# Another order of the 36 steps of the routed experts, with the single-expert steps spread among the others

## The chip, the cores and the metric

The kernel runs on one core of a Trainium2 chip. The metric is the device time of one execution in microseconds (us), median of the runs shown. Engines: PE multiplies (PEld loads its stationary operand), DVE and ACT do elementwise work, POOL (GpSimd) issues the indirect transfers of this stage, SP issues the transfers of the dense weights.

## The reference, cut to what matters

Two blocks of a network run one after the other on 256 tokens of width 1024. The change lies in the routed experts of the first block:

```
_, e_idx = lax.top_k(jnp.where(expert_mask, biased, -jnp.inf), TOP_K)     # 8 of 64 experts for each of 256 tokens
...
def expert_block(args):
    xb, e = args
    return (jax.nn.silu(xb @ w_gate[e]) * (xb @ w_up[e])) @ w_down[e]
...
routed = jax.ops.segment_sum(yb * row_gate[:, None], row_tok, num_segments=T + 1)[:T]
```

An expert's gate and up weights are 1024 x 512 numbers together (2.10 MB in f32), its down weights 256 x 1024 (1.05 MB), 3.15 MB in all. There are 2048 pairs of token and expert. Evaluating the reference's routing on its own inputs gives these token counts, sorted: 157, 93, 91, 88, 86, 82, 73, 65, 59, 56, 53, 49, and so on down to 1, 1, 0, 0. So two experts have no token, and one has more than 128.

## The kernel before, in words

**Steps and sets.** The routed experts are computed in 36 steps of 128 rows each. Experts are ranked by their token count while the kernel runs, and a *set* is one expert's weights in one of six buffers. A *solo* step (S, 8 of them) gives all 128 rows to one of the 8 best-filled experts: one set. A *mixed* step (X, 16) holds one expert of ranks 8 to 23 in 64 rows, one of ranks 24 to 39 in 32 rows, and 32 rows for an overflow: three sets. A *narrow* step (Z, 12) holds two experts of ranks 40 to 63 and two overflows, in 32 rows each: four sets. That makes 104 sets. Whether an overflow is used depends on the data: an expert gets overflow rows only for tokens beyond its 128, 64 or 32 rows. With the counts above only one overflow is used (the expert with 157 tokens), and it is the first overflow, which belongs to the first mixed step. The requests for the other 39 overflow sets and for the two experts without tokens are issued all the same, but every index in them is out of bounds, so they move no weights. The two experts without tokens are those of the last narrow step. So a step moves this many experts' weights: solo 1, mixed 2 (the first one 3), narrow 2 (the last one 0), 63 in all.

**What sets the order.** The string `ORDER` (L116) gives the kind of each step; `sets_of(i)` says which weights step i uses, and set number s goes to buffer s % 6 (`SETS = 6`). `row_of(i)` maps a step to its column in the tables, and the host writes the table of row bases in `_route` from the same string.

**POOL's queue** (L720, L724, L712). Ahead of the loop, sets 0, 1, 2, then 5 and 3, then 4 are requested, and the rows of steps 0 to 2. Then for each step i, in this order: the rows of step i + 3 (`gather`, L712, once the rows of step i have been turned); after PE has done gate and up of step i, gate and up of the sets that reuse that step's buffers (`after_step(i)`, L720); after PE has done down of step i - 1, the down weights of the sets that reuse those (L724). All requests are served in the order in which they are issued.

**PE's order in a step** (L1137, L1156, L1170, L1123, L915): gate and up of step i (waits for all its sets, and for ACT and DVE to have copied the turned rows, L1844 and L2767), down of step i - 1, combine of step i - 2, turning the rows of step i + 1, turning the hidden values of step i. ACT's silu of step i (L1860) comes once in a step, right after gate and up.

```
if after_step(i):
    full(pool, "moe", mu("gu", i))
for s in after_step(i):
    gate_up(s)
```

Of the kernel before, what the change touches and what calls it, by code (L numbers as in the profile page):

```python
# [112 lines left out]
STEPS, W_UNITS, OVER = FIRST_STEP["end"], FIRST_UNIT["end"], FIRST_UNIT["end"] - EXPERTS  # L113
GROUP = 32
SETS = 6
ORDER = [{"S": "solo", "X": "mixed", "Z": "narrow"}[c] for c in "SSZSZSZXXXZZZZXXXXXSZSZZZSZSXXXXXXXX"]  # L116
UNUSED = float(1 << 20)


def row_of(i):  # L120

    return FIRST_STEP[ORDER[i]] + ORDER[:i].count(ORDER[i])


def sets_of(i):

    n = ORDER[:i].count(ORDER[i])
    pair, quad, over = (FIRST_UNIT[name] for name in ("pair", "quad", "over"))
    mixed, narrow = FIRST_STEP["narrow"] - FIRST_STEP["mixed"], STEPS - FIRST_STEP["narrow"]
    return {"solo": [n], "mixed": [pair + n, quad + n, over + n],  # L130
            "narrow": [quad + mixed + 2 * n, quad + mixed + 2 * n + 1, over + mixed + narrow + n, over + mixed + n]}[ORDER[i]]


def groups_of(i):

    cuts = {"solo": [(0, 0, P)], "mixed": [(0, 0, 32), (0, 32, 64), (1, 64, 96), (2, 96, P)],
            "narrow": [(h, GROUP * h, GROUP * h + GROUP) for h in range(4)]}[ORDER[i]]
    return [(first_of(i) + h, slice(at, end)) for h, at, end in cuts]
# [5 lines left out]
def first_of(i):  # L144

    return FIRSTS[i]
# [3141 lines left out]
def _route(np):  # L3288
# [7 lines left out]
    for i in range(STEPS):  # L3296
        for unit, col in {"solo": ((0, 0),), "mixed": ((0, 0), (1, 2 * GROUP)), "narrow": ((0, 0), (1, GROUP))}[ORDER[i]]:
            c[:, ROUTE["base"] + sets_of(i)[unit]] = P * row_of(i) + col
# [66 lines left out]
```

## Time and profile before

| | |
|---|---|
| median of 3 runs | 1881.57 us (1877.88 to 1883.33) |
| profiled execution: its span | 1885.5 us |
| routed steps, first gate and up to last combine | about 534 to 1082 us of the span |
| PE busy over the span | 93% |
| bytes of the software queue (POOL) | 218.10 MB of 414.50 MB |

Of the profiled execution only the span is given. It is 3.9 us over the median of the runs and 2.2 us over the slowest of them. The page has 40 slices of 47.1 us; the routed steps are slices 11 to 23. A time in the rows is counted from the start of the span.

### The profile page before, as it was taken

The numbers are of one execution on the slowest core, as the hardware profiler recorded it, in microseconds if no ns is written. First come the engines' busy times: TensorE is split into PE (matmuls) and PEld (weight loads), VectorE is DVE, ScalarE is ACT, GpSimd is POOL, SyncE is SP. The second block draws the span as 40 slices with busy tenths as digits, with TensorE's granted clock in tenths as the row PEclk, the third lists the DMA queues.
The fourth block names the chain that finished last, engine by engine and source line by source line (L and its number), as shares of the span: only waits on it lengthen the run. The fifth ranks groups of instructions, "written<-read, shape, count | busy, mean of one in ns | idle before, by whom it ended". The sixth has DMA issues, their size and how long they took to land.

```text
span 1885.5 us, 30512 instructions
## 1 busy us (share of the span) xinstructions
PE 1744.2 (93%) x12794; PEld 1265.1 (67%) x12794; DVE 920.3 (49%) x1354; ACT 668.3 (35%) x948; POOL 498.7 (26%) x360
## 2 busy tenths in 40 slices
PE   6999999999899888999998989899997979979998
PEld 3899998786454333444444467678886749968887
DVE  4276933766732111112121378565447775765453
ACT  3455347443311111111111255454434452334442
POOL 1277877100134344434544200000000002400000
PEclk9999999999889998999999989999998989989999
DMA  8455541156689999998799933155554400024542
GB/s 363 180 183 189 187 179 68 67 225 237 271 319 374 388 391 377 390 418 340 267 380 409 396 120 132 67 207 189 200 198 143 172 23 26 4 90 179 180 174 91
DMA packets 64700, 414.50 MB, mean 220 GB/s; under 512 B 20308, under 2 KB 20340, under 8 KB 24256
## 3 DMA queue, kind: packets, MB, share of 16 engines
q0 software_dynamic: 37536, 218.10, 29.3%
q1 hardware_dynamic: 26624, 192.95, 27.6%
q8 instruction: 95, 1.56, 0.3%
q10 hardware_dynamic: 416, 1.66, 0.2%
q14 instruction: 29, 0.24, 0.0%
HBM read 549.99 MB, written 2.10 MB: 293 GB/s over the span
## 4 chain that ended last, share of the span: by engine, by line
PE 78%; DVE 10%; issue 3%; DMA 3%; ACT 2%; another core or an unknown queue 1%; POOL 1%; ACTq 0%; DVEq 0%; POOLq 0%
PE ps L1137 13%; PE ps L827 10%; PE ps L829 10%; PE ps L828 10%; PE ps L1156 6%; PE ps L868 5%; PE ps L869 5%; PE ps L870 5%; PE ps L1170 3%; PE ps L1535 3%; DMA arena<-in_moe_dn,arena 2%; PE ps L886 2%; PE ps L1123 1%; DVE ring_lo L2352 1%; PE ps L1571 1%
## 5 line engine op out<-in xcount | busy, mean ns | idle before, releaser
L828 PE MATMUL ps<-ring_lo,arena_r 128*128 128x512 f32 x888 | 349.4, 393 | 0.0
L1137 PE MATMUL ps<-arena 128*32 128x512 f32 (+1 forms) x896 | 244.0, 614 | 10.3 <-ACT arena L1844 6.1
L1137 PE MATMUL ps<-ring,arena 128*32 128x512 f32 (+1 forms) x752 | 230.0, 614 | 16.8 <-issue 8.7
L870 PE MATMUL ps<-arena_r,ring_lo 128*128 128x256 f32 x768 | 217.3, 283 | 0.0
L827 PE MATMUL ps<-arena_r 128*128 128x512 f32 x528 | 209.5, 397 | 2.7 <-DVE arena_r L2378 2.7
L829 PE MATMUL ps<-arena_r 128*128 128x512 f32 x528 | 206.1, 390 | 0.0
L828 PEld LDWEIGHTS ps<-ring_lo,arena_r 128*128 128x128 f32 x888 | 169.1, 190 | 33.5
L2352 DVE TENSOR_TENSOR ring_lo<-ring,arena_r 128x2048 fp32r<-128x2048 f32 x66 | 150.7, 2291 | 75.2 <-ACT arena_r L1722 75.1
L1722 ACT ACTIVATE high<-ring 128x2048 fp32r<-128x2048 f32 x62 | 118.5, 1915 | 117.2 <-PE ps L868 71.7
L868 PE MATMUL ps<-arena_r,high 128*128 128x256 f32 x528 | 150.9, 286 | 2.4 <-DVE ring_lo L2352 1.3
L869 PE MATMUL ps<-arena_r,high 128*128 128x256 f32 x528 | 149.4, 283 | 0.0
L870 PEld LDWEIGHTS ps<-arena_r,ring_lo 128*128 128x128 f32 x768 | 147.4, 192 | 0.0
L2792 DVE SCALAR_TENSOR_TENSOR arena<-ps,arena 128x256 f32<-128x256 f32 x36 | 17.4, 484 | 262.6 <-ACT arena L1860 262.6
L661 POOL TENSOR_TENSOR ring_lo<-ring,high 128x2048 fp32r<-128x2048 f32 x26 | 120.5, 4634 | 86.6 <-ACT high L1722 86.6
L1722 ACT ACTIVATE arena_r<-ring 128x2048 fp32r<-128x2048 f32 x66 | 126.1, 1920 | 37.6 <-DMA ring<-in_weights 37.6
L1156 PE MATMUL ps<-arena 128*32 128x512 f32 (+1 forms) x448 | 124.2, 620 | 6.7 <-DMA arena<-in_moe_dn,arena 6.7
L1137 PEld LDWEIGHTS ps<-ring,arena 128*32 128x32 f32 (+1 forms) x752 | 66.2, 118 | 94.5 <-issue 93.0
L1137 PE MATMUL ps<-spare,arena 128*32 128x512 f32 x272 | 123.7, 607 | 0.5
L1156 PE MATMUL ps<-ring,arena 128*32 128x512 f32 (+1 forms) x376 | 117.1, 607 | 0.9 <-ACT arena L1868 0.5
L1137 PEld LDWEIGHTS ps<-arena 128*32 128x32 f32 (+1 forms) x896 | 71.2, 120 | 69.8 <-issue 69.7
L827 PEld LDWEIGHTS ps<-arena_r 128*128 128x128 f32 x528 | 99.2, 188 | 22.4 <-issue 3.2
L829 PEld LDWEIGHTS ps<-arena_r 128*128 128x128 f32 x528 | 99.1, 188 | 20.8
(490 smaller groups left out, 3551.7 us busy)
## 6 DMA issues: line engine op xcount, KB each, us to landing
ring<-in_weights SPq DMA_DIRECT2D x183, 1024.0 KB, 4.8
arena<-in_ln POOLq DMA_DIRECT2D x2, 1024.0 KB, 5.1
arena<-in_lora POOLq DMA_DIRECT2D x1, 1152.0 KB, 5.5
arena<-in_x POOLq DMA_DIRECT2D x1, 1024.0 KB, 12.4
h_rows<-arena ACTq DMA_DIRECT2D x1, 1024.0 KB, 12.0
arena<-in_bands POOLq DMA_DIRECT2D x1, 1024.0 KB, 7.5
arena<-in_rw_kk_ka POOLq DMA_DIRECT2D x2, 512.0 KB, 7.8
arena<-in_rw_w0a POOLq DMA_DIRECT2D x1, 1024.0 KB, 4.9
```

The costliest lines, as they stand in the source:

```text
L661: pool.tensor_tensor(ring_lo[:, s, :], ring[:, s, :], hi_of(stage, i).bitcast(F32), ALU.subtract).then_inc(sem(f"w_split{s}"), 1)
L827: head = pe.matmul(dst, hi, w, start=start, stop=False, skip_group_check=True)
L828: pe.matmul(dst, hi, rest, start=False, stop=False, skip_group_check=True)
L829: return head, pe.matmul(dst, lo, w, start=False, stop=stop, skip_group_check=True)
L868: head = pe.matmul(dst, w, hi[:, k, :], start=(k == 0), stop=False)
L869: pe.matmul(dst, w, lo[:, k, :], start=False, stop=False)
L870: mm = pe.matmul(dst, rest, hi[:, k, :], start=False, stop=(k == count - 1))
L1137: mm = pe.matmul(pb("moe", mu("gu", i))[at, :], x_cols[:, k, at], gu_w[s % SETS][:, k * 512:(k + 1) * 512], start=(k == 0), stop=(k == KC ...
L1156: mm = pe.matmul(pb("moe", mu("y", i, n))[at, :], hid_cols[:, i % 2, f, at], dn_w[s % SETS][:, f * D + n * 512:f * D + n * 512 + 512], sta ...
L1170: mm = pe.matmul(ps[:, 2 * t + n, :], places_of[:, i % 2, tokens(t)], part[:, i % 2, n * 512:(n + 1) * 512], start=False, stop=(i == STEPS ...
L1722: fn(hi_of(stage, i), ring[:, s, :], ACT.Copy).then_inc(sem(f"w_hi{s}"), 1)
L2352: tt(ring_lo[:, s, :], ring[:, s, :], hi_of(stage, i).bitcast(F32), S).then_inc(sem(f"w_split{s}"), 1)
```

## The change

The string that gives the kinds of the steps is another one. It has the same 8 S, 16 X and 12 Z. Requests, buffers and products are made by the same code.

```diff
-ORDER = [{"S": "solo", "X": "mixed", "Z": "narrow"}[c] for c in "SSZSZSZXXXZZZZXXXXXSZSZZZSZSXXXXXXXX"]
+ORDER = [{"S": "solo", "X": "mixed", "Z": "narrow"}[c] for c in "SSXXXXSZSZSZXXXSZSZZZZXXXSZZZZXXXXXX"]
```

With the position of each step (0 to 35), the experts whose weights each moves, and a vertical bar every six steps:

```
before  kinds    S S Z S Z S | Z X X X Z Z | Z Z X X X X | X S Z S Z Z | Z S Z S X X | X X X X X X
before  experts  1 1 2 1 2 1 | 2 3 2 2 2 2 | 2 2 2 2 2 2 | 2 1 2 1 2 2 | 2 1 0 1 2 2 | 2 2 2 2 2 2
after   kinds    S S X X X X | S Z S Z S Z | X X X S Z S | Z Z Z Z X X | X S Z Z Z Z | X X X X X X
after   experts  1 1 3 2 2 2 | 1 2 1 2 1 2 | 2 2 2 1 2 1 | 2 2 2 2 2 2 | 2 1 2 2 2 0 | 2 2 2 2 2 2
```

Three places show what moves. On POOL, early in the loop: what is requested after gate and up of step 2, before the change. `in_moe_gu` are gate and up weights, `in_moe_dn` down weights, `h_rows` the gathered token rows; `ring`, `spare`, `arena` and `twin` are where the buffers lie.

```order
L720 DMA ring<-in_moe_gu,arena 128x4096
L720 DMA spare<-in_moe_gu,arena 128x4096
L720 DMA arena<-in_moe_gu,arena 128x4096
L720 DMA ring<-in_moe_gu,arena 128x4096
L724 DMA arena<-in_moe_dn,arena 128x2048
L712 DMA arena<-h_rows,arena 128x1024
L720 DMA arena<-in_moe_gu,arena 128x4096
```

After the change, at the same place:

```order
L720 DMA ring<-in_moe_gu,arena 128x4096
L720 DMA spare<-in_moe_gu,arena 128x4096
L720 DMA arena<-in_moe_gu,arena 128x4096
L724 DMA arena<-in_moe_dn,arena 128x2048
L712 DMA arena<-h_rows,arena 128x1024
L720 DMA ring<-in_moe_gu,arena 128x4096
L720 DMA arena<-in_moe_gu,arena 128x4096 x2
```

Step 2 gave four buffers back and now gives three; of the three requests two carry weights (of the four, two did), and step 3 gives back three instead of one.

On POOL, later: from the request for the rows of step 22 to that for the rows of step 24 (it lies after gate and up of step 20), before the change, where step 19 is solo.

```order
L712 DMA arena<-h_rows,arena 128x1024
L720 DMA ring<-in_moe_gu,arena 128x4096
L724 DMA ring<-in_moe_dn,arena 128x2048
L724 DMA arena<-in_moe_dn,arena 128x2048 x2
L712 DMA arena<-h_rows,arena 128x1024
L720 DMA spare<-in_moe_gu,arena 128x4096
L720 DMA arena<-in_moe_gu,arena 128x4096
L720 DMA ring<-in_moe_gu,arena 128x4096
L720 DMA arena<-in_moe_gu,arena 128x4096
L724 DMA ring<-in_moe_dn,arena 128x2048
L712 DMA arena<-h_rows,arena 128x1024
```

After the change, from the same request on, where step 19 is the second of four narrow steps in a row.

```order
L712 DMA arena<-h_rows,arena 128x1024
L720 DMA arena<-in_moe_gu,arena 128x4096 x2
L720 DMA ring<-in_moe_gu,arena 128x4096
L720 DMA spare<-in_moe_gu,arena 128x4096
L724 DMA ring<-in_moe_dn,arena 128x2048
L724 DMA twin<-in_moe_dn,arena 128x2048
L724 DMA arena<-in_moe_dn,arena 128x2048
L724 DMA ring<-in_moe_dn,arena 128x2048
L712 DMA arena<-h_rows,arena 128x1024
```

The solo step gave back one buffer and the narrow step gives back four of gate and up; the down requests behind them are four, where they were three (of mixed step 18).

On PE, from the turning of step 19's rows on, before (one expert's weights for all 128 rows, then down of the mixed step 18):

```order
L1123 MATMUL ps<-cst,arena 128x128 x8
L915 MATMUL ps<-cst,arena 128x128 x2
L1137 MATMUL ps<-ring,arena 128x512 x8
L1156 MATMUL ps<-ring,arena 32x512 x2
L1156 MATMUL ps<-arena 32x512 x2
```

After, the same place is the narrow step 19:

```order
L1123 MATMUL ps<-cst,arena 128x128 x8
L915 MATMUL ps<-cst,arena 128x128 x2
L1137 MATMUL ps<-arena 32x512 x2
L1137 MATMUL ps<-ring,arena 32x512
L1137 MATMUL ps<-spare,arena 32x512
L1137 MATMUL ps<-arena 32x512 x2
```

PE's work of a step changes its form with the kind; DVE and ACT have the same instructions in the same order in both kernels.

## Rows read from the trace of the kernel before

**Rows 1.** The page: clock of PE and share of transfers, in tenths, 40 slices.

```profile
PEclk9999999999889998999999989999998989989999
DMA  8455541156689999998799933155554400024542
```

**Rows 2.** Transfers by queue (packets, MB, share), 500 to 1090 us.

```profile
q0 software_dynamic: 35582, 209.19, 89.5%
```

**Rows 3.** Stretches of the routed steps: length, busy time by engine, PEclk, DMA share, GB/s.

```profile
534.00:563.00 29.00, 28.48 (x129) 12.63 (x128) 4.90 (x11) 4.57 (x10) 8.89 (x9) 0.97 0.81 313
563.00:604.00 41.00, 40.62 (x198) 19.70 (x196) 8.90 (x18) 7.41 (x15) 17.80 (x18) 1.00 0.91 349
604.00:701.00 97.00, 87.68 (x661) 38.53 (x660) 17.92 (x36) 15.37 (x30) 41.54 (x42) 0.96 0.97 389
701.00:774.00 73.00, 62.94 (x457) 25.95 (x456) 12.05 (x24) 10.43 (x21) 34.65 (x35) 0.88 0.95 376
774.00:835.00 61.00, 56.81 (x412) 26.06 (x416) 12.10 (x24) 10.31 (x21) 27.68 (x28) 0.97 1.01 416
835.00:890.00 55.00, 54.50 (x364) 25.42 (x360) 11.91 (x24) 9.98 (x20) 22.74 (x23) 1.00 0.91 355
890.00:950.00 60.00, 56.41 (x344) 26.30 (x339) 11.85 (x24) 10.31 (x21) 29.68 (x30) 1.00 0.80 297
950.00:978.00 28.00, 27.75 (x212) 12.67 (x208) 6.03 (x12) 5.42 (x11) 10.89 (x11) 1.00 0.90 365
978.00:1068.00 90.00, 83.71 (x689) 39.56 (x684) 17.93 (x36) 15.36 (x31) 35.71 (x37) 0.98 1.00 408
```

**Rows 4.** Timeline of ACT, L1860: steps 2, 6, 7, 11, 15, 19, 29, 35.

```profile
562.73 0.38 ACT L1860 ACTIVATE arena<-ps 128x256 f32<-128x256 f32 x1 [7.04 <-PE ps L1137]
...
618.16 0.38 ACT L1860 ACTIVATE arena<-ps 128x256 f32<-128x256 f32 x1 [6.84 <-PE ps L1137]
636.74 0.39 ACT L1860 ACTIVATE arena<-ps 128x256 f32<-128x256 f32 x1 [11.64 <-PE ps L1137]
...
701.06 0.38 ACT L1860 ACTIVATE arena<-ps 128x256 f32<-128x256 f32 x1 [6.10 <-PE ps L1137]
...
773.81 0.39 ACT L1860 ACTIVATE arena<-ps 128x256 f32<-128x256 f32 x1 [6.66 <-PE ps L1137]
...
834.74 0.38 ACT L1860 ACTIVATE arena<-ps 128x256 f32<-128x256 f32 x1 [7.71 <-PE ps L1137]
...
977.63 0.39 ACT L1860 ACTIVATE arena<-ps 128x256 f32<-128x256 f32 x1 [6.83 <-PE ps L1137]
...
1067.64 0.38 ACT L1860 ACTIVATE arena<-ps 128x256 f32<-128x256 f32 x1 [6.84 <-PE ps L1137]
```

**Rows 5.** The chain that ended last, 611 to 637 us (start, duration).

```profile
611.03 7.11 PE ps L1137 x64
618.91 8.76 DMA arena<-in_moe_gu,arena
627.91 8.80 PE ps L1137 x64
```

**Rows 6.** Why PE sat idle ahead of instructions that write ps, 534 to 1082 us.

```profile
  ACT arena L1844: 13.0, 9
  issue: 8.7, 5
  DMA arena<-in_moe_dn,arena: 7.2, 4
  DMA arena<-in_moe_gu,arena: 3.2, 1
```

**Rows 7.** Timeline of POOL ahead of the loop: first and last weight requests.

```profile
504.30 1.06 POOL L720 DMA_INDIRECT arena<-in_moe_gu,arena  x1 [66.82 <-DVE arena L2418]
...
535.52 0.99 POOL L720 DMA_INDIRECT arena<-in_moe_gu,arena  x1 [0.30 <-issue]
```

**Rows 8.** Timeline of PE: where gate and up of step 2 begins.

```profile
555.59 0.62 PE L1137 MATMUL ps<-ring,arena 128*32 128x512 f32 x1 [0.32 <-DVE last_r L2776]
```

## Prediction

> **What bounds the kernel now.** I read the page first: the clock of PE is near full over the whole span, and the transfer row stands at 8 to 9 tenths in slices 11 to 23, the routed steps, and falls only around slice 20 [rows 1]. So in this stage PE and the transfers are both nearly full, and the question is where the one waits for the other. The timeline of ACT gives the length of each step, since silu comes once in a step. From step 2 to step 6 it is 55.43 us for four steps, 13.86 us each, with PE busy almost throughout: that is the step's floor, for solo and narrow steps alike, since both issue the same length of work. Against this floor steps 7 to 19 take 216.58 us instead of 180.2 (36.4 lost), steps 20 to 29 take 142.89 instead of 138.6 (4.3 lost) and steps 30 to 35 take 90.01 instead of 83.2 (6.8 lost) [rows 4]. In all 47.5 us are lost, nearly all inside the two long rows of steps without a solo step.
>
> What the transfers could give shows in the bytes and the stretches. POOL's queue moved 209.2 MB between 500 and 1090 us [rows 2]; 63 experts of 3.146 MB are 198.2, the gathered rows of 2048 pairs 8.4, and the rest is parameters. In the stretches where the transfers never rested they moved 408 to 416 GB/s [rows 3]. The share that they rested, times the stretch, is 0.19 x 29 + 0.09 x 41 = 9.2 us before 604 us, 0.03 x 97 + 0.05 x 73 = 6.6 us from 604 to 774, and 0.09 x 55 + 0.20 x 60 + 0.10 x 28 = 19.8 us from 835 to 978 [rows 3]: 35.6 us of idle transfers in a stage that loses 47.5 us. The first 9.2 us are idle because steps 0 to 6 ask for 10 experts in 7 steps and the buffers are full; right after them PE stands for twelve steps in a row for lack of weights. That idle time is what another order can win.
>
> **The balance of one step.** A step with two experts needs 2 x 3.146 MB at 416 GB/s, 15.1 us, and 8.4 MB / 36 of gathered rows, 0.5 us: 15.6 us, 1.7 us more than the 13.86 of PE. A solo step needs 8.1 and gives 5.7 us back. The overflow set adds 7.6 us in the first mixed step. The last narrow step moves nothing but rows and gives 13.3 back. The loads can run ahead only so far: a buffer comes free when gate and up of its step end, its next user (two steps on) starts 13.86 + 6.84 = 20.7 us later, and between lie 0.75 us to POOL's issue, another 1.3 for the second request, and 8.76 us from issue to arrival, as in the chain at 618.91 us [rows 4, 5], with 5.0 us for the second expert behind the first where both wait in the queue. That is 15.8 us, so the lead is 5 to 6 us; I take 6.
>
> Keeping that lead step by step for the order before, from 6 at step 6 on: step 7 loses 3.3 and each of steps 8 to 18 loses 1.7 (22.0), steps 31 to 35 lose 7.6, and what the solo steps and the empty step give beyond a lead of 6 is idle transfer time, 23.3 us from step 19 on. The trace has 36.4, 6.8 and 19.8 us for these. So the account has the places right, is fair on the idle time (0.85 of it is real) and short on PE's loss in the long row.
>
> **The change, part by part.** No instruction is added or removed by kind: the same 8, 16 and 12 steps, the same 63 experts, the same products on PE. Costs there are zero, and so are those of DVE, ACT and SP; the last six steps are mixed in both orders, so what follows the stage comes as before. What moves is when two-expert steps ask.
>
> 1. *Steps 0 to 5 become 1 1 3 2 2 2.* The overflow set is now requested ahead of the loop, as set 4, last of all. Ahead of gate and up of step 2 lie in the queue five whole experts and the gate and up of a sixth set, 5 x 7.56 + 5.0 = 42.8 us, and the rows of three steps, 1.7 us or, since the first steps are the fullest, up to 3. They start about 2 us after the first request at 504.30 us; the last is issued at 535.52 us and is not the limit [rows 7]. Arrival is 551 to 553 us, and PE comes to step 2 at 555.6 us [rows 8]. Loss 0, or 1 us at the 313 GB/s at which this stretch ran so far in part; I take 1. The 9.2 us of idle transfers before 604 us shrink to about 1: **-8.2 us**.
> 2. *The third expert of the first mixed step.* Before, it was issued at 618.91 us for the very next step and PE stood 3.2 us, after which gate and up took 8.80 us instead of 7.11 because the clock had dropped to its half level [rows 5, 6]. This place is gone; it is part of the sum of item 1.
> 3. *Steps 6 to 35.* The same account from a lead of 6 at step 2 gives the lead 0.9 at step 5, and never empty until step 14 (0.8 lost). Steps 18 to 24 are seven two-expert steps in a row: 0.8 at step 21 and 1.7 each at 22, 23, 24, 5.9 lost. The last steps 33 to 35 lose 4.2. Idle transfer time is 0.6 + 4.0 + 4.0 at solo steps 6, 8 and 10, 3.7 at 17 and 7.9 at the empty step 29: 20.2 us against 23.3 before; at 0.85 that is 17.2 against 19.8: **-2.6 us**.
> 4. *The 6.6 us of short rests* between 604 and 774 us come from waits that free a buffer late; I leave them: 0.
> 5. *Waits that the transfers do not explain by name.* PE sat 13.0 us for ACT's copy of turned rows and 8.7 us for nothing that the trace names [rows 6]. By the timeline most of them lie in the stretches where the transfers never rest, 604 to 835 and 978 to 1068 us, 321 us long: 0.068 us per us. Nothing shows their cause, so I bound them: nothing (if they are a sign of PE waiting for weights anyway), or at this rate over the longer busy stretch of the new order. Restful stretches were 213 us; the new order rests at steps 6 to 10, 17 and 29, about 155 us. 58 x 0.068 = **+4.0 us**. I take it in full.
>
> Sum: -8.2 - 2.6 + 4.0 = -6.8 us. Against the profiled execution, 1885.5 - 6.8 = 1878.7 us of span; the median of the runs shown is 3.9 us less than that span, so 1881.6 - 6.8 = **1874.8 us**, say 1875. The sum over idle transfers, not that over PE's waits (29.6 - 11.9 = 17.7 us less), is taken, because both orders end with the same six steps and the end of the loads sets their time.
>
> After a wait PE ran at 1.2 instead of 2.4 GHz: the stretch from 701 to 774 us has a mean clock of 0.88, the worst of the stage [rows 3]. Nothing in the sum needs more than the rows. The Trainium skill (TensorE: Matmul & The Clock Gate, Part 1: The HAM clock gate) says that PE's default is the half rate and that activity releases it; the trace agrees with 8.80 us for work that takes 7.11. By this rule every wait removed gives back more than itself, which speaks for a larger gain, the rival below.
>
> **A rule that speaks against the change.** In busy stretches 408 to 416 GB/s were moved [rows 3]. The Trainium skill (DMA: Bandwidth & Descriptors, Specifications) gives about 358 GB/s as the limit of memory for one core. By that figure the 206.6 MB would take 577 us, more than the whole stage has, no order would leave the transfers idle, and no order could win anything. The trace contradicts it, since one core alone moved more for 61 us on end. The sum does not use it.
>
> **The rivals.**
>
> *A larger gain* (chance 0.18): the unnamed waits are PE's hunger for weights in another dress, and go with it. Then item 5 is 0 and PE's waits shrink as the account says: between -10.8 and -17.7 us, 1868 at the middle. For it: they stand in the long rows of two-expert steps. Against: one of them stands at the edge of a restful stretch, and ACT's copy doesn't depend on weights at all.
>
> *No difference* (0.30): given back in steps 18 to 24. In the order before, the account had 22.0 us for steps 7 to 18 and the trace 36.4, 1.65 times as much. If the new losses (11.9) grow likewise, to 19.7, and the longer run empties the lead earlier, most of the 6.8 is gone: about 1881 us, within 5.6.
>
> *Slower* (0.16): four narrow steps in a row. A narrow step gives back four buffers, two of which then hold nothing, so only four of six carry weights and POOL spends its issues of 1.3 us on empty requests. The only such place before, steps 10 to 13, lies in and ahead of the worst stretch: share 0.95, 376 GB/s, clock 0.88 [rows 3], where steps 12 to 15 take 72.8 us instead of 55.4, 4.3 us lost a step [rows 4]. The new order has two, 18 to 21 (followed by three mixed) and 26 to 29. If steps 20 to 24, those behind the used-up lead, lose 4.3 us each, that is 21.5 us where I count 5.9, and the sum turns to -6.8 + 15.6 = +8.8 us: 1890 us. It decides from 18 us lost there.
>
> *The change does nothing by itself* is excluded: requests, not only names, move.
>
> **How the numbers follow.** The forecast, 5.6 to 11 us faster, has 0.36. A measurement of this kernel can tell about 0.3%, 5.6 us. Faster by more than that: 0.36 + 0.18 = 0.54; within: 0.30; slower: 0.16. The range goes from 1866 (into the larger gain) to 1888 (into the slower case) and leaves out about one in ten on either side. The forecast's own range is 1871 to 1876.
>
> **What would show each step right or wrong.** Right: DMA share 0.97 or more from 534 to 604 us; no wait for `in_moe_gu` over 1 us at step 2; silu of step 11 at about 563.7 + 9 x 13.86 = 688 us, where before it came at 701 [rows 4]; a rest of the transfers near 950 us; 15 to 25 us lost between steps 18 and 24 at most. Wrong: a wait at step 2 over 3 us, an idle share before 604 us as before, more waits of the unnamed kind than 26 us, or over 18 us lost in steps 18 to 24.

## The result and the profile after

| | before | after |
|---|---|---|
| median, runs side by side | 1880.05 us (1877.88 to 1883.33, 4 runs) | 1869.13 us (1867.67 to 1869.43, 4 runs) |
| ratio, 95% interval | | 0.9946 (0.9929 to 0.9964) |
| profiled execution: span | 1885.5 us | 1866.6 us |

The change makes the kernel faster by 0.54%, 10.2 us of 1880.05, with an interval of 6.8 to 13.3 us. The two profiled spans differ by more, 18.9 us, since the profiled execution of before was above its own runs; that of after was not (its run took 1868.89 us). So the traces tell where time went, and the ratio how much. One of six further runs of the changed kernel, in after_again below, took 2344.45 us at a granted clock of 0.70, where the other five took 1862.59 to 1870.93, and it is left out of that ratio.

The page of the changed kernel first: granted clock and transfers, 40 slices of 46.7 us.

```profile
PEclk8999999999889999999999999999998989989999
DMA  9555552166699999899879832354454400024442
```

In the routed steps, slices 11 to 23, the clock's 8 in slice 16 has gone, and slice 12 of the transfers, the first whole one of the stage, reads 9 for 8 [rows 1]. The bytes are the same, to 0.01 MB [rows 2]. The stretches are those of [rows 3], with the same columns; the last one ends with silu of step 35, here as there:

```profile
534.00:563.00 29.00, 28.48 (x129) 12.37 (x128) 4.49 (x10) 4.41 (x10) 8.74 (x10) 1.00 1.00 421
563.00:604.00 41.00, 40.00 (x329) 19.91 (x331) 8.91 (x18) 7.46 (x15) 18.07 (x19) 1.00 0.97 391
604.00:701.00 97.00, 95.61 (x585) 45.26 (x580) 20.55 (x42) 17.91 (x35) 41.21 (x42) 1.00 0.96 384
701.00:774.00 73.00, 69.33 (x445) 32.16 (x438) 14.82 (x30) 12.41 (x24) 32.65 (x33) 0.98 0.98 400
774.00:835.00 61.00, 57.29 (x434) 24.88 (x432) 11.91 (x24) 10.30 (x21) 29.67 (x30) 1.00 0.92 359
835.00:890.00 55.00, 49.81 (x392) 22.56 (x392) 11.28 (x23) 9.79 (x19) 28.68 (x29) 0.97 1.01 417
890.00:950.00 60.00, 56.15 (x388) 25.94 (x392) 12.55 (x25) 10.23 (x20) 27.91 (x29) 1.00 0.79 304
950.00:978.00 28.00, 27.02 (x206) 10.25 (x207) 3.56 (x8) 3.92 (x8) 13.51 (x14) 0.94 0.85 337
978.00:1047.00 69.00, 65.56 (x546) 30.06 (x538) 14.51 (x29) 11.81 (x23) 27.80 (x29) 1.00 1.01 417
```

Two things are to be read here. The last two columns of the first two rows are 1.00 at 421 GB/s and 0.97 at 391, where before they were 0.81 and 0.91: the transfers rest 1.2 us before 604 us, not 9.2. And PE's busy time, the first column behind the length, is 95.6 of 97 and 69.3 of 73 us in the third and fourth rows, where it was 87.7 and 62.9 [rows 3]. The time won is there.

All rests together (what is missing to a share of 1.00, times the length, up to 978 us) fell from 35.6 to 28.2 us, by 7.4. That is less than the 18.4 us of lost time that the next rows give: the busy transfers also moved more at the end, 417 GB/s from 978 to 1047 us, where before they moved 408 from 978 to 1068 [rows 3]. No run tests why.

The steps, by the timeline of ACT (silu of steps 2, 11, 17, 20, 22, 24, 29 and 35):

```profile
560.90 0.38 ACT L1860 ACTIVATE arena<-ps 128x256 f32<-128x256 f32 x1 [7.04 <-PE ps L1137]
...
686.60 0.38 ACT L1860 ACTIVATE arena<-ps 128x256 f32<-128x256 f32 x1 [6.83 <-PE ps L1137]
...
774.83 0.38 ACT L1860 ACTIVATE arena<-ps 128x256 f32<-128x256 f32 x1 [6.84 <-PE ps L1137]
...
818.92 0.38 ACT L1860 ACTIVATE arena<-ps 128x256 f32<-128x256 f32 x1 [7.39 <-PE ps L1137]
...
853.20 0.38 ACT L1860 ACTIVATE arena<-ps 128x256 f32<-128x256 f32 x1 [6.83 <-PE ps L1137]
...
882.86 0.39 ACT L1860 ACTIVATE arena<-ps 128x256 f32<-128x256 f32 x1 [6.83 <-PE ps L1137]
...
958.71 0.38 ACT L1860 ACTIVATE arena<-ps 128x256 f32<-128x256 f32 x1 [7.72 <-PE ps L1137]
...
1047.40 0.38 ACT L1860 ACTIVATE arena<-ps 128x256 f32<-128x256 f32 x1 [6.83 <-PE ps L1137]
```

Against the floor of 13.86 us a step, steps 3 to 17 lose 213.93 - 207.9 = 6.0 us, steps 18 to 24 lose 108.03 - 97.0 = 11.0, and steps 25 to 35 lose 164.54 - 152.5 = 12.1: 29.1 us in all, 18.4 less than the 47.5 of before [rows 4]. Outside the steps the two traces hardly differ: the stage begins 1.8 us earlier and what follows it takes 1.3 us more, so 18.4 + 1.8 - 1.3 = 18.9 us, the whole difference of the spans.

Last, why PE sat idle from 534 us to the end of the stage, as in [rows 6]:

```profile
  DMA arena<-in_moe_dn,arena: 8.0, 4
  ACT arena L1844: 4.8, 6
  issue: 3.7, 8
  DMA twin<-in_moe_dn,arena: 2.0, 1
  DMA ring<-in_moe_dn,arena: 1.4, 1
  DMA arena<-in_moe_gu,arena: 0.8, 1
```

The waits that name a transfer are 12.2 us, where they were 10.4. What fell are the two rows that name none, ACT's copy and "issue": from 21.7 to 8.5 us [rows 6]. So of the 47.5 us lost before, waits that name a transfer hold only 10.4, and the prediction's "for lack of weights" covered more than its rows say.

### The profile page after: what moved, and what is told of

Its sections match the earlier page's. It is cut to its first block, busy times and chain, and to the rows that moved or that the text cites. A ratio compares the mean times of both kernels' runs of the same rounds, so it can differ in the third digit from the quotient of the medians.

```text
span 1866.6 us, 30512 instructions
## 1 busy us (share of the span) xinstructions
PE 1735.7 (93%) x12794; PEld 1262.0 (68%) x12794; DVE 920.6 (49%) x1354; ACT 667.9 (36%) x948; POOL 498.6 (27%) x360
## 3 DMA queue, kind: packets, MB, share of 16 engines
q0 software_dynamic: 37536, 218.10, 29.1%
## 4 chain that ended last, share of the span: by engine, by line
PE 77%; DVE 10%; DMA 4%; issue 3%; ACT 2%; POOL 1%; another core or an unknown queue 0%; ACTq 0%; DVEq 0%; POOLq 0%
PE ps L1137 11%; PE ps L827 10%; PE ps L828 10%; PE ps L829 10%; PE ps L1156 6%; PE ps L868 5%; PE ps L870 5%; PE ps L869 5%; DMA arena<-in_moe_dn,arena 3%; PE ps L1170 3%; PE ps L1535 3%; PE ps L886 2%; PE ps L1123 1%; DVE ring_lo L2352 1%; PE ps L1571 1%
## 5 line engine op out<-in xcount | busy, mean ns | idle before, releaser
L1137 PE MATMUL ps<-arena 128*32 128x512 f32 (+1 forms) x880 | 238.4, 601 | 5.4 <-ACT arena L1844 2.1
L1137 PE MATMUL ps<-ring,arena 128*32 128x512 f32 (+1 forms) x752 | 215.4, 596 | 5.4 <-ACT arena L1844 2.4
L1156 PE MATMUL ps<-arena 128*32 128x512 f32 (+1 forms) x440 | 123.1, 616 | 6.0 <-DMA arena<-in_moe_dn,arena 2.6
L1137 PE MATMUL ps<-spare,arena 128*32 128x512 f32 (+1 forms) x288 | 120.7, 594 | 1.6 <-issue 1.0
L1156 PE MATMUL ps<-ring,arena 128*32 128x512 f32 (+1 forms) x376 | 112.8, 609 | 6.0 <-DMA arena<-in_moe_dn,arena 5.4
L1137 PEld LDWEIGHTS ps<-ring,arena 128*32 128x32 f32 (+1 forms) x752 | 62.2, 113 | 80.3 <-issue 79.6
## 6 DMA issues: line engine op xcount, KB each, us to landing
arena<-in_x POOLq DMA_DIRECT2D x1, 1024.0 KB, 12.4
```

Of the source, the lines that this page charges most:

```text
L1137: mm = pe.matmul(pb("moe", mu("gu", i))[at, :], x_cols[:, k, at], gu_w[s % SETS][:, k * 512:(k + 1) * 512], start=(k == 0), stop=(k == KC ...
L1156: mm = pe.matmul(pb("moe", mu("y", i, n))[at, :], hid_cols[:, i % 2, f, at], dn_w[s % SETS][:, f * D + n * 512:f * D + n * 512 + 512], sta ...
```

## The experiments

The twelve runs were made on three chips, and a ratio holds against the runs of before on the same chip: 1889.74 us median on the first, 1877.56 on the second, 1879.36 on the third. "Lost" is the time of steps 3 to 35 over 33 x 13.86 us; "unnamed" is PE idle for ACT's copy L1844 and "issue". Both come from the one profiled execution. That of over_first took 1874.17 us, the shortest of its 12 runs, whose median is 1886.96: its lost time is no measure of what the order is worth.

| kernel | chip | ratio (95%) | span, us | lost | unnamed |
|---|---|---|---|---|---|
| before_again | 1 | single run, 1889.91 us | 1887.6 | 49.6 | 28.5 |
| over_first | 1 | 0.9981 (0.9962 to 1.0001) | 1872.0 | 33.6 | 11.4 |
| early_fill | 1 | 0.9968 (0.9947 to 0.9988) | 1878.1 | 38.0 | 12.2 |
| alternate | 1 | 0.9963 (0.9945 to 0.9982) | 1877.5 | 41.4 | 19.9 |
| after_again | 2 | 0.9934 (0.9915 to 0.9953) | 1866.5 | 23.9 | 0.2 |
| empty_late | 2 | 0.9926 (0.9911 to 0.9942) | 1860.1 | 23.2 | 0 |
| no_weights | 2 | single run, 1839.61 us | 1837.8 | -2.1 | 0 |
| no_weights_after | 2 | single run, 1835.34 us | 1833.5 | -1.8 | 0 |
| over_first_2 | 3 | 0.9976 (0.9959 to 0.9993) | 1875.0 | 32.6 | 12.0 |
| after_3 | 3 | 0.9953 (0.9937 to 0.9969) | 1869.8 | 28.3 | 9.8 |
| only_gu | 3 | single run, 1866.24 us | 1864.4 | 26.1 | 7.7 |
| only_dn | 3 | single run, 1856.42 us | 1854.6 | 14.7 | 9.3 |

**before_again.** The kernel before, a second profile, to see whether its unnamed waits are its own.

> The kernel before, unchanged, profiled once more. The two profiled executions differ by 18.9 us (1885.5 against 1866.6), the medians by 10.9. Theory A (transfer account: the order sets idle transfers and waits for weights, the waits without a named cause come and go with the execution): span of 1875 to 1880 us, again 3 to 4 us of wait for weights and half-rate PE at step 7, the same twelve steps too long, DMA share of about 0.81 and 0.91 before 604 us, but clearly less than the 21.7 us of waits for ACT L1844 and for nothing named. Theory B (those waits belong to the order before): again about 20 us of them and a span near 1885 us.

Measured: 28.5 us unnamed, and the long steps at the same places: step 7 took 18.48 us (18.58 before), step 19 17.58 (17.56), step 24 17.31 (17.32). This is what Theory B expected. The long steps and their waits come back in a second execution.

**over_first and over_first_2.** Only steps 2 and 7 exchanged, so that the three experts of the first mixed step are asked for ahead of the loop.

```diff
-"SSZSZSZXXXZZZZXXXXXSZSZZZSZSXXXXXXXX"
+"SSXSZSZZXXZZZZXXXXXSZSZZZSZSXXXXXXXX"
```

> Order before, with the kinds of steps 2 and 7 exchanged alone (SSXSZSZZ...): the first mixed step, the one that needs a third expert, comes at step 2. The long row of two-expert steps 6 to 18 stays. Theory A (idle transfers at the start are filled, PE then stands later as the account says): 5 to 6 us faster than before, half of the gain of the changed order; step 7 near 14 us, steps 8 to 18 still lose 1.7 us and more each. Theory B (the gain is the removed wait of step 7 with its slow clock, nothing else): the whole 10 us. Theory C (the balance of the whole stage sets its end, the place of one set does not matter): within 2 us of before.

> The order before with steps 2 and 7 exchanged, again, on a chip that also times the whole change. Theory A (the early filling and the overflow's early place are most of the gain): 0.995 to 0.997, at least half of what the whole change gains. Theory B (the solo steps spread among the others matter as much): 0.998, under a third of the gain of the whole change.

Measured: 0.9981 on chip 1, 0.9976 on chip 3, where the whole change gave 0.9953. That is 3.6 and 4.5 us faster, a little under the 5 to 6 of Theory A of over_first and far from the 10 of Theory B, though on chip 1 the interval still touches no gain. By these medians one exchange of two steps is worth 2.4/4.7, half of the change; the intervals (0.7 to 4.1 and 3.1 to 6.3 in a thousand) leave room for anything between a ninth and the whole. Step 7, 18.58 us before, took 13.75 and 13.77 us, but the next ones of the long row (steps 8, 9 and 11 to 14 on chip 3) still took 15.8 to 18.9. The share fits the first theory of over_first_2, the ratio is nearer to the 0.998 of the second, and the interval holds both. What is left of the gain must come from what follows, more two-expert steps early and solo steps between the rest; how it divides between these is not shown.

**early_fill.** Steps 0 to 14 as in the change, but with the four narrow steps right behind the three mixed ones.

```diff
-"SSZSZSZXXXZZZZXXXXXSZSZZZSZSXXXXXXXX"
+"SSXXXXSZSZSZXXXZZZZXXXXXSZSZZZSZXXXX"
```

> Starts as the changed order (SSXXXXSZSZSZ, steps 0 to 11), then a row of twelve two-expert steps without a solo step as in the order before, then solo and narrow steps and four mixed ones (SSXXXXSZSZSZXXXZZZZXXXXXSZSZZZSZXXXX). It tells the early filling from the spreading of solo steps. Theory A (transfer account): waits of about 12 x 1.7 - 6 = 14 us in steps 12 to 23, last solo steps and the empty step leave idle transfers of 15 us or more; 5 to 9 us faster than before, 1 to 4 us slower than the changed order. Theory B (a long row costs 36 us as it did in the profiled execution of before, and only spreading helps): no faster than before.

**alternate.** The change with its first four narrow steps taken apart, so that narrow and mixed steps alternate.

```diff
-"SSXXXXSZSZSZXXXSZSZZZZXXXSZZZZXXXXXX"
+"SSXXXXSZSZSZXXXSZSZXZXZXZSZZZZXXXXXX"
```

> Changed order, with steps 18 to 24 as ZXZXZXZ instead of ZZZZXXX; nothing else differs and each of the seven still moves two experts. Theory A (only the number of experts of a step counts): within 2 us of the changed order, 8 to 12 us faster than before, 17 to 20 us lost in steps 18 to 24 as in the changed order. Theory B (four narrow steps in a row are bad, since two of their four buffers hold nothing): 3 us or more faster than the changed order. Theory C (what counts is how many real sets have to be handed over between neighbouring kinds: a mixed step behind a narrow one finds its pair of sets released in one go): 1 to 4 us slower than the changed order.

Measured: 0.9968 and 0.9963, no different from each other. early_fill, 6.0 us faster than before, keeps thirteen two-expert steps in a row (11 to 23), as many as before (6 to 18), and gains all the same, as its Theory A expected; its Theory B, that only spreading helps, falls. In that row steps 16 to 18 took 18.02, 16.38 and 18.51 us. In alternate steps 18 to 24 lost 895.16 - 782.64 - 97.0 = 15.5 us, where the change with its four narrow steps in a row lost 11.0 there (on another chip; the change itself was not run on chip 1). So nothing speaks for the rival that four narrow steps in a row are what costs. Both kernels also lost time in steps 4 to 6 on this chip, 6.4 and 8.1 us, where the change lost 0 and 0.9 on chips 2 and 3. The account has its thinnest lead here (0.9 us at step 5), but that is not what the rows show: in neither kernel does a wait in these steps name a transfer. In steps 5 and 6 of alternate, 17.56 us each, the first down result comes 1.77 us after silu, as in an undisturbed step, and the copy of the turned rows at 7.99 and 7.98 us where it is usually at 5.89. This is the lateness shown under only_dn below.

**after_again and after_3.** The changed kernel, twice more.

> The changed order, unchanged, beside the others of this call. Theory A (the gain is real and comes from weights that arrive in time): 0.5 to 0.7% faster than before, with at most 15 us of waits for ACT L1844 and nothing named, where two profiles of before had 22 and 28. Theory B (good luck of the first execution): under 0.3% faster, waits without a named transfer of 20 us or more.

> The changed kernel a third time, beside over_first_2 on the same chip. From the two results so far 0.993 to 0.996; unnamed waits under 10 us and lost time in steps 3 to 35 of 23 to 30 us.

Measured: 0.9934 and 0.9953, as expected, so with the first pair three measurements agree on 9 to 12 us. The unnamed waits were 0.2 us in one execution and 9.8 in the other with the same program. In after_again the lost time was 23.9 us, nearly all behind waits that name a transfer (down weights 15.9 us, gate and up 2.8, rows 3.9). In the first pair's profile and in after_3 the named waits were 12.2 and 15.3 us, yet the lost time only 5.2 and 4.4 us more than there. It looks as if fewer waits for weights are left where the unnamed ones are many; no run tests it.

**empty_late.** Another order with the same kinds, which by the prediction's account would leave the transfers less idle still; the step that moves nothing is now step 33.

```diff
-"SSXXXXSZSZSZXXXSZSZZZZXXXSZZZZXXXXXX"
+"SZSZSXXSZSZXZZZZXZZXXXXSZSXXXXXXSZXX"
```

> Another order (SZSZSXXSZSZXZZZZXZZXXXXSZSXXXXXXSZXX), made by the transfer account with both traces: solo and narrow steps alternate at the start, the last narrow step, which moves no weights, comes at step 33, so that its 13 us of unused transfer time are not needed in the middle. Theory A (transfer account): 3 to 5 us faster than the changed order, 12 to 16 us faster than before, and the last weights land some 10 us earlier than there. Theory B (the place of the empty step does not matter; rows of two-expert steps, here 6 to 8 long, decide): within 2 us of the changed order, or slower.

Measured: 0.9926 (0.9911 to 0.9942), against 0.9934 (0.9915 to 0.9953) for the change on the same chip: the lowest median of the kernels that compute everything (1863.49 us, the change on this chip 1867.17), but the intervals lie over each other. Theory A had expected it 3 to 5 us faster than the change. The stretches of its trace, for 563 to 604, 604 to 701, 774 to 835 and 835 to 890 us:

```profile
563.00:604.00 41.00, 40.63 (x260) 18.79 (x253) 8.86 (x18) 7.67 (x15) 17.17 (x19) 1.00 0.99 406
604.00:701.00 97.00, 95.08 (x629) 44.34 (x627) 20.87 (x43) 17.92 (x35) 42.74 (x44) 1.00 0.98 394
...
774.00:835.00 61.00, 52.42 (x435) 23.54 (x436) 11.27 (x23) 9.64 (x19) 31.05 (x32) 1.00 0.99 404
835.00:890.00 55.00, 54.51 (x407) 24.89 (x398) 11.42 (x23) 9.95 (x20) 24.32 (x25) 1.00 1.02 419
```

From 563 to 978 us the transfers are never under 0.98; they rest at the start (0.78 before 563 us) and in the last stretch (0.87 from 978 to 1056). So the order does what the account asks. It beats the kernel before clearly. A further gain over the change is not shown.

**no_weights and no_weights_after.** Both orders with the routed experts' weights left out: every request is issued, next to no index is in bounds (POOL's queue moved 11.11 MB, not 209.19), and the products use what the buffers hold. Their times show the stage without weight transfers, and the routed output is not computed.

```diff
 pool.indirect_dma_start(gu_w[s % SETS], None, a["moe_gu"], rows_at(s),
-                        bounds_check=EXPERTS * P - 1,
+                        bounds_check=0,
...
 pool.indirect_dma_start(dn_w[s % SETS], None, a["moe_dn"], rows_at(s),
-                        bounds_check=EXPERTS * P - 1,
+                        bounds_check=0,
```

> Order before, but the bound of the indices of the expert weights is 0, so that no expert's weights are moved (all requests, waits and products stay; the routed experts' result is left out). It measures the floor of PE and the waits that do not come from transfers. Theory A (all lost time of steps 2 to 35 comes from weight transfers, the unnamed waits too): each step 13.8 us, 0 to 3 us lost instead of 47.5, span about 47 us shorter, no waits for ACT L1844. Theory B (the waits for ACT L1844 and for nothing named are PE's or ACT's own, or POOL's issues'): they stay, 10 to 20 us lost.

> The same with the changed order: the routed experts' weights are not moved. Theory A: the same time as with the order before, within 2 us, since the order is worth nothing without transfers. Theory B (the order also changes PE's own time, through the forms of its products): a difference of more than 3 us.

Measured: steps 3 to 35 take 13.75 to 13.95 us each in both, and steps 1 to 35 together 475.65 and 475.91 us. Without weights the order is worth nothing, POOL's 1.3 us for each of 208 weight requests limit nothing, and the whole of the lost time is gone, on this chip, where the kernels with weights had next to no unnamed waits either. The two runs differ by 4.3 us, more than the 3 that Theory B asked for, but this lies ahead of the stage (silu of step 0 at 542.38 and 537.80 us).

**only_gu and only_dn.** The order before with one of the two left out: the down weights (140.5 MB move), or gate and up (74.4 MB). The routed output is not computed in them either. Each has one half of the diff above.

> The order before, with the down weights of the routed experts left out (no index of their requests is in bounds), so the transfers of the stage fall from 206.6 to 140.5 MB. It tells apart what the unnamed waits are (21.7 and 28.5 us in the two profiles of before, 0 where no weights move). Theory A: PE's hunger for weights in another dress. With 140.5 MB, 10.7 us of transfers for a step of two experts against 13.86 of PE, nobody is hungry any more and the unnamed waits are under 2 us, the lost time under 5 us. Theory B: the moving itself disturbs PE or the copies, in proportion to the bytes. Then two thirds of the unnamed waits stay, 14 to 19 us.

> The order before, with the gate and up weights of the routed experts left out, so 74.4 MB move. Theory A: unnamed waits under 2 us. Theory B: a third of them stays, 7 to 10 us.

Measured: with 140.5 MB 7.7 us are unnamed, with 74.4 MB 9.3 us. For only_dn this is the 7 to 10 us of Theory B, but in only_gu Theory B expected 14 to 19, so the waits are not in proportion to the bytes; Theory A expected under 2 in both. It is not hunger, at least in only_dn (in only_gu 9.1 us of waits still name a transfer): in only_dn the transfers were busy for 0.35 to 0.46 of the time up to 835 us, no wait named a transfer, and yet steps 11 to 14 took 18.24, 16.65, 15.81 and 17.63 us. What it looks like shows when step 11 of only_dn is laid beside the same step of no_weights, both from the silu of step 10 on (timeline of ACT). First no_weights:

```profile
673.19 0.39 ACT L1860 ACTIVATE arena<-ps 128x256 f32<-128x256 f32 x1 [6.83 <-PE ps L1137]
674.96 0.60 ACT L1852 ACTIVATE arena_r<-ps 128x512 fp32r<-128x512 f32 x1 [1.39 <-PE ps L1156]
676.62 0.60 ACT L1852 ACTIVATE arena_r<-ps 128x512 fp32r<-128x512 f32 x1 [1.06 <-PE ps L1156]
679.08 0.60 ACT L1844 ACTIVATE arena<-ps 128x512 f32<-128x512 f32 x1 [1.86 <-PE ps L1123]
...
686.95 0.39 ACT L1860 ACTIVATE arena<-ps 128x256 f32<-128x256 f32 x1 [6.83 <-PE ps L1137]
```

Then only_dn:

```profile
673.03 0.39 ACT L1860 ACTIVATE arena<-ps 128x256 f32<-128x256 f32 x1 [6.83 <-PE ps L1137]
674.80 0.60 ACT L1852 ACTIVATE arena_r<-ps 128x512 fp32r<-128x512 f32 x1 [1.39 <-PE ps L1156]
677.47 0.60 ACT L1852 ACTIVATE arena_r<-ps 128x512 fp32r<-128x512 f32 x1 [2.07 <-PE ps L1156]
681.76 0.60 ACT L1844 ACTIVATE arena<-ps 128x512 f32<-128x512 f32 x1 [3.69 <-remote]
...
691.27 0.39 ACT L1860 ACTIVATE arena<-ps 128x256 f32<-128x256 f32 x1 [7.65 <-PE ps L1137]
```

Counted from the silu at the top, what ACT gets from PE comes 0.00, 1.01, 2.84 and 4.48 us later in only_dn. The lateness doesn't come at one instant, as behind a wait; it grows over the down products, the combine and the turning, 2.84 us within 6.96 us (674.80 to 681.76). So "PE idle for ACT L1844" is PE waiting for the copy of its own late result. PE's rows of only_dn don't show it coming:

```profile
678.29 1.03 PE L1123 MATMUL ps<-cst,arena 128*128 128x128 f32 x8
679.16 0.38 PE L915 MATMUL ps<-cst,arena 128*128 128x128 f32 x2
682.50 1.03 PE L1137 MATMUL ps<-ring,arena 128*32 128x512 f32 x1 [2.96 <-ACT arena L1844]
```

The turning begins 5.26 us after silu, exactly as in no_weights, and then PE stands for 2.96 us. Either PE was slow and its rows (whose ends are modelled) ran ahead of it, or its results were held up on their way to ACT and DVE. For a slow PE speaks what follows: from 682.50 us its rows of gate and up lie 0.86 us apart, where 0.43 is usual. But it is argued and not shown. The granted clock of only_dn reads full up to that point (length, busy time by engine, PEclk, DMA share, GB/s):

```profile
676.00:679.00 3.00, 3.00 (x19) 2.27 (x16) 1.09 (x4) 0.60 (x1) 2.39 (x3) 1.00 0.09 6
679.00:682.00 3.00, 0.55 (x5) 0.30 (x3) 0.18 (x1) 0.24 (x1) 2.39 (x3) 1.00 0.25 36
682.00:685.00 3.00, 2.50 (x12) 0.69 (x16) 0.69 (x1) 0.74 (x2) 1.01 (x2) 0.57 0.87 352
```

It stands at full speed up to 682 us and then falls to 0.57, PE's lower level for most of that row, at a time when the transfers (the last two columns) had been nearly idle until then. No long wait lay ahead of it: steps 3 to 10 of only_dn took 13.77 to 13.93 us each.

## Why the prediction was right, and where it was not

The forecast, 1874.8 us, was in the right direction and 5.7 us too long; 1.5 of these are the reference (1881.57 us when it was made, 1880.05 side by side).

**Right: what the order acts on.** Idle transfers early, and PE waiting later. Without weights the lost time is gone in both orders (on chip 2); with them, the order that fills early is faster in three measurements. Not all of the later loss is hunger, as item 5 below shows.

**Right: item 1.** The rest before 604 us was to shrink from 9.2 to about 1 us; it is 0.00 x 29 + 0.03 x 41 = 1.2 us. No wait for gate and up stands ahead of step 2; its first product waited 0.32 us for DVE, as before [rows 8]. Silu of step 11 was forecast at 688 us and came at 686.60.

**Right: item 2.** The stand at the overflow's set is gone, and over_first shows it alone: step 7 took 13.75 us, where it was 18.58, and 18.48 on the same chip.

**Item 3, not borne out.** It named -2.6 us for less rest of the transfers behind step 5. From 835 to 978 us they rest 0.21 x 60 + 0.15 x 28 = 16.8 us where they rested 19.8, which is -3.0; but 0.08 x 61 = 4.9 us of rest are new from 774 to 835 us, where the row before showed none [rows 3]. Together that is 1.9 us more rest. From 604 to 774 us, item 4, it is 5.3 us for 6.6. The lost time of steps 18 to 24 was put at 5.9 us and is 11.0, and 12.1 us were lost from step 25 on, most of it in steps 28 to 32 and not in 33 to 35. The long row before was short by a factor 1.65 in the account, and the new rows are short by 1.9 and more. The account's lead is generous: its own rows give 20.7 - 15.8 = 4.9 us, and it took 6. It also has no term for late results, and in the first pair's trace both are in the loss.

**Wrong: item 5.** This is the term that failed most clearly. The unnamed waits were taken to grow with the busy stretches, +4.0 us. They fell, from 21.7 to 8.5 us in the first pair of profiles, and to 0.2 and 9.8 in the two others. With item 5 at nothing the prediction's own sum is -8.2 - 2.6 = -10.8 us, and 10.2 (6.8 to 13.3) were measured. That the two are so close is in part luck: item 3 did not come, and the fall of the unnamed waits stands in no term. The rival of a larger gain had -10.8 as its lower edge. But its reason, that these waits are hunger for weights, doesn't hold for only_dn, which has 9.3 us of them and no wait for a transfer. They are stretches in which PE's results come late. Why there are fewer in the new order was not shown: over_first, with the long row nearly intact, also had only 11.4 and 12.0. Nor is it shown how the gain divides between fuller transfers and fewer late results. after_again gained 12.4 us with 0.2 us of unnamed waits; but the kernel before was not profiled on that chip, and whether it had more of them there is open.

**Rivals.** "No difference" asked that the losses of the new order grow from 11.9 to 19.7 us. They did, to 29.1, of which 11.0 in steps 18 to 24, and the change won all the same: against them stand not the 29.6 us of the account but the 47.5 of the trace. "Slower" asked for over 18 us in steps 18 to 24; the three profiles of the change have 11.0, 11.5 and 12.6, and alternate without the four narrow steps in a row was no better.

**Which of two sums.** The prediction took the sum over idle transfers and set aside the one over PE's waits, -17.7. By the first pair of profiles the lost time fell by 18.4 us, close to the second. By the runs side by side it is 10.2, close to the first. The profiled execution of before was a long one, and a sum that is measured against it gets its excess as a gain.

## What to carry to other kernels

Where a queue of transfers and an engine are both nearly full, write down bytes and engine time for each step, and look for the place where the transfers rest: work that needs more bytes than time belongs there, above all ahead of a long hungry stretch, and one exchange of two steps may already bring a good part of the gain. Before a wait without a plausible releaser is priced, lay the same step beside an undisturbed one, row by row: lateness that comes at one row is a wait, lateness that grows over several rows is something else, whatever the releaser's column says. And measure a gain by runs side by side, since the excess of one profiled execution looks like something that can be won.

## What the runs showed of the hardware

- **PE's results can come late while the granted clock reads full.** In the kernel before, step 24 took 17.32 us. The rows of ACT (timeline, silu of step 23 to silu of step 24):

```profile
890.15 0.39 ACT L1860 ACTIVATE arena<-ps 128x256 f32<-128x256 f32 x1 [6.84 <-PE ps L1137]
...
898.16 0.60 ACT L1844 ACTIVATE arena<-ps 128x512 f32<-128x512 f32 x1 [3.77 <-remote]
...
907.47 0.39 ACT L1860 ACTIVATE arena<-ps 128x256 f32<-128x256 f32 x1 [6.09 <-PE ps L1137]
```

  The copy comes 8.01 us after silu, where it is 5.89 in no_weights, though PE's rows have the turning at its usual place, 5.27 us after silu (895.42). Then gate and up, which began at once behind it (898.90), ended 8.57 us later, where the same work takes 7.14 from 555.59 to 562.73 us [rows 4, 8], with PE busy nearly throughout and the clock at 1.00 (the columns of [rows 3]):

```profile
899.00:901.00 2.00, 2.00 (x20) 0.68 (x23) 0.69 (x1) 0.01 (x1) 1.65 (x2) 1.00 1.05 418
901.00:904.00 3.00, 2.89 (x26) 0.87 (x22) 0.00 (x0) 0.38 (x1) 0.99 (x1) 1.00 1.01 342
904.00:907.00 3.00, 3.00 (x32) 1.17 (x29) 0.00 (x0) 0.00 (x0) 0.00 (x0) 1.00 0.86 328
```

  The Trainium skill (TensorE: Matmul & The Clock Gate, Part 1: The HAM clock gate) warns that the trace's records of the clock have been seen to be unreliable on this generation; if it is PE that is slow here, these rows agree. What makes the results late stays open. None of the four kernels on chip 2 showed it, all eight on chips 1 and 3 did. The chip may have a part in it, but two of the four moved no weights, the order before with its weights was not among them, and each kernel has one profile there; so that no_weights had none can't be put down to the missing weights either. The Trainium skill says on the same page, of kernels on three or more cores of a die, that a limiter of peak current slows dense matmuls and that zeroed inputs escape it. No run here tests that for one core.
- **One core moved 421 GB/s** from 534 to 563 us with the transfers busy throughout, above the 408 to 416 of [rows 3].
- **A request without a valid index costs POOL what a full one does,** 0.99 us and 0.30 us to the next in no_weights, as for the requests of before that move weights [rows 7], and 208 of them in a stage of 500 us limited nothing.
